# Two-layer decoder trunk: the prompt attention's fill bank is copied out in another order, its second query unit is taken out in two pieces, and some pooling products move into the last head pair

## The reference, cut to what matters

```python
pv, pg, c_q, c_kv, k_r, ag, mg_pool, mg_attn = split_in(x @ w_in)
b_pool = pool_branch(v_ext, pos, pg, pool_w, pool_scale) @ pool_up
q_nope, q_rope, lat, k_rope = mla_qk(c_q, c_kv, k_r, pos, ...)
o = mla_prompt(...)  # or mla_sample(...)
b_attn = (o * jax.nn.silu(ag)) @ attn_up
sub = (sigmoid(mg_pool) * b_pool + sigmoid(mg_attn) * b_attn) @ w_out
return layer_norm(DN_ALPHA * x + sub + sigmoid(x @ ple_gate) * (p_i @ ple_proj), ln_g, ln_b)
```

## Time and profile before

| what | value |
|---|---|
| three executions | 2037.77, 2044.54, 2045.38 us (median 2044.54) |
| the profiled execution | 2032.2 us, its span 2030.4 us |
| instructions | 31146 |
| PE busy | 1912.3 us (94%) |
| DVE, POOL, ACT busy | 905.2, 737.0, 565.4 us |
| mean granted clock of TensorE | 0.98 |

### The profile page before, as it was taken

The page is one execution under the profiler, slowest core; times in us unless marked ns, Lnnn a source line. Parts: engine busy times, 40 slices in busy tenths (PEclk is TensorE's granted clock), DMA queues, the critical chain, the costliest instruction groups (busy, mean ns, idle before and its releaser), DMA issues.

```text
span 2030.4 us, 31146 instructions
## 1 busy us (share of the span) xinstructions
PE 1912.3 (94%) x12391; PEld 1816.3 (89%) x12391; DVE 905.2 (45%) x1484; ACT 565.4 (28%) x997; POOL 737.0 (36%) x743
## 2 busy tenths in 40 slices
PE   6999899999999999999989989999999999999994
PEld 5998888888799999999989968888878999999994
DVE  4344566664164111535454535666623721134216
ACT  6123444443122010201251334444421310120002
POOL 3332343342145333434244322343312443334434
PEclk9999999999999999999999999999999899999997
DMA  5213221053812221222132141121365122222222
GB/s 212 74 47 131 65 64 62 22 177 123 288 34 62 78 66 56 89 89 68 30 128 55 41 165 33 55 64 61 138 234 181 32 89 72 67 68 87 66 67 84
DMA packets 94746, 183.96 MB, mean 91 GB/s; under 512 B 12086, under 2 KB 35942, under 8 KB 93964
## 3 DMA queue, kind: packets, MB, share of 16 engines
q1 hardware_dynamic: 73440, 135.43, 21.7%
q10 hardware_dynamic: 21180, 46.80, 6.1%
HBM read 150.19 MB, written 32.45 MB: 90 GB/s over the span
## 4 chain that ended last, share of the span: by engine, by line
PE 73%; DVE 11%; ACT 9%; issue 3%; ACTq 1%; DMA 1%; POOL 1%; DVEq 0%; SPq 0%; POOLq 0%
PE PS L615 52%; PE PS L710 5%; PE PS L638 4%; PE PS L595 4%; DVE MX L1662 3%; ACT PB L1243 2%; ACT PTH L1047 2%; DVE PTL L1650 2%; PE PS L695 2%; PE PS L730 1%; PE PS L671 1%; DVE PS L1661 1%; PE PS L754 1%; DMA RAW<-in_wstream 1%; ACT FST L1047 1%
## 5 line engine op out<-in xcount | busy, mean ns | idle before, releaser
L512 POOL CAST WH<-RAW 128x512 fp32r<-128x512 f32 (+3 forms) x292 | 200.7, 687 | 905.8 <-DMA RAW<-in_wstream 905.8
L514 POOL TENSOR_TENSOR WL<-RAW,WH 128x512 fp32r<-128x512 f32 (+3 forms) x292 | 382.2, 1309 | 23.5
L615 PE MATMUL PS<-XH,WH 128*128 128x344 f32 x1344 | 290.0, 324 | 4.6 <-ACT SGB L1283 3.9
L615 PE MATMUL PS<-XL,WH 128*128 128x344 f32 x1344 | 287.4, 322 | 0.0
L615 PE MATMUL PS<-XH,WL 128*128 128x344 f32 x1344 | 286.8, 322 | 0.0
L615 PEld LDWEIGHTS PS<-XH,WH 128*128 128x128 f32 x1344 | 228.0, 190 | 7.3 <-ACT SGB L1283 4.5
L615 PEld LDWEIGHTS PS<-XH,WL 128*128 128x128 f32 x1344 | 227.5, 189 | 0.0
L615 PEld LDWEIGHTS PS<-XL,WH 128*128 128x128 f32 x1344 | 227.3, 190 | 0.0
L533 POOL TENSOR_SCALAR PB<-PB,RC 128x128 f32<-128x128 f32 (+7 forms) x128 | 96.1, 751 | 333.3 <-DVE RC L1644 333.3
L638 PE MATMUL PS<-XH,WH 128*128 128x344 f32 x384 | 127.4, 332 | 29.1 <-ACT FST L1047 29.1
L1243 ACT ACTIVATE PB<-PS,NB 128x128 f32<-128x128 f32 (+7 forms) x128 | 95.0, 742 | 188.2 <-DVE NB L1663 187.9
(11 more groups left out here) (275 smaller groups left out, 3860.2 us busy)
## 6 DMA issues: line engine op xcount, KB each, us to landing
RAW<-in_wstream SPq DMA_DIRECT2D x236, 256.0 KB, 2.7
PAGES<-in_pages SPq DMA_DIRECT2D x128, 320.0 KB, 4.9
spill_p<-PST ACTq DMA_DIRECT2D x16, 516.0 KB, 2.9
spill_g<-FST ACTq DMA_DIRECT2D x48, 172.0 KB, 1.9
SGL<-spill_g ACTq DMA_DIRECT2D x16, 516.0 KB, 4.4
PRJ<-spill_p ACTq DMA_DIRECT2D x16, 516.0 KB, 4.4
spill_v<-VSTG ACTq DMA_DIRECT2D x16, 512.0 KB, 2.8
VSP<-spill_v SPq DMA_DIRECT2D x8, 1024.0 KB, 5.3
```

The costliest lines, as they stand in the source:

```text
L512: pool.tensor_copy(WH[:, slot, 0:size], RAW[:, slot, 0:size]).then_inc(w_high[slot], 1)
L514: pool.tensor_tensor(WL[:, slot, 0:size], RAW[:, slot, 0:size], f(WH[:, slot, 0:size]), ALU.subtract).then_inc(w_split[slot], 1)
L615: last = nc.tensor.matmul(PS[:, 3 * par + c, 0:CH], w[:, slot, at], x(k)[:, c * CH:(c + 1) * CH], start=(k == 0 and n == 0), stop=(k == kt ...
```

## The change

The second query unit's third bank (344 columns) is multiplied first and counts `q_rot` alone; then the banks 0 and 1 (688 columns) in a second instruction. PE waits for the first of them, runs the first 8 fill matmuls, fill(-2), ahead of scores(1), and the other 16 behind it. The fill bank's chunks are copied on ACT in the steps 2, 4, 7, 10, 13, 16 and not 2, 5, 8, 11, 14, 16; chunk 0 ahead of PTH(0) and not behind it. The spill DMA is issued behind exp(n). In the last pair of a layer 14 of the 24 pooling products stand ahead of values(7).

```diff
-        PV_FIRST = 24
+        PV_HEAD, PV_FIRST = 14, 24
-        FILL_AT = {-1: (0, 24)} | {n: (24 + 8 * n, 32 + 8 * n) for n in range(15)}
-        FILL_EVAC = {2: 0, 5: 1, 8: 2, 11: 3, 14: 4, 16: 5}
+        FILL_AT = {-2: (0, 8), -1: (8, 24)} | {n: (24 + 8 * n, 32 + 8 * n) for n in range(15)}
+        FILL_EVAC = {2: 0, 4: 1, 7: 2, 10: 3, 13: 4, 16: 5}
...
                     scores(l, i, 0)
+                    pe.wait_ge(q_rot, 3 * r + 2)
+                    fill(l, i, -2)
                     scores(l, i, 1)
                     fill(l, i, -1)
...
                     if i < PAIRS - 1:
                         keys_unit(i + 1)
+                    else:
+                        pv_fill(l, (0, PV_HEAD))
                     values(r, GROUPS - 1)
...
-                pv_fill(l, (0, PV_FIRST))
+                pv_fill(l, (PV_HEAD, PV_FIRST))
...
                     copy(FST[:, b, :], PS[:, FILL_BANK, 0:CH]).then_inc(fill_free, 1)
+
+                def fill_spill(l, i, chunk):
+
+                    r, b, c = l * PAIRS + i, chunk % 2, chunk % 3
                     act.wait_ge(fill_free, 6 * r + chunk + 1)
-                    c = chunk % 3
                     act.dma_start(SPILL_G[...], FST[:, b, :]).then_inc(fill_out[b], 16)
...
-                        act.wait_ge(q_rot, 2 * r + h + 1)
+                        act.wait_ge(q_rot, 3 * r + 2 * h + 1)
...
                     for n in range(18):
                         m = n - 2
+                        if n == 2:
+                            fill_evac(l, i, 0)
...
-                        if n in FILL_EVAC:
+                        if n in FILL_EVAC and n > 2:
                             fill_evac(l, i, FILL_EVAC[n])
                         if n < 16:
...
+                        if n in FILL_EVAC:
+                            fill_spill(l, i, FILL_EVAC[n])
...
-                        own(v.tensor_tensor(thirds(QRAW[:]), bank_set(1 - h), thirds(TAB[:]), ALU.mult))
+                        if h == 0:
+                            own(v.tensor_tensor(thirds(QRAW[:]), bank_set(1), thirds(TAB[:]), ALU.mult))
+                        else:
+                            v.tensor_tensor(QRAW[:, 2 * CH:T], PS[:, FILL_BANK, 0:CH], TAB[:, 2 * CH:T], ALU.mult
+                                            ).then_inc(q_rot, 1)
+                            own(v.tensor_tensor(thirds(QRAW[:])[:, 0:2, :], bank_set(0)[:, 0:2, :], thirds(TAB[:])[:, 0:2, :],
+                                                ALU.mult))
+                            dve.wait_ge(q_rot, 3 * r + 2)
```

## The result

The changed kernel takes **2015.3 us** (median of 4, 2008.9 to 2019.7) beside 2041.2 for the kernel before: ratio 0.9875, 95% interval 0.9845 to 0.9904. Two later comparisons gave 0.9877 (0.9843 to 0.9912; 2015.8 beside 2037.8) and 0.9881 (0.9857 to 0.9905; 2012.0 beside 2037.3). It is 22 to 26 us faster. The kernel before had come out lower too: 2041.2 here and 2035.9 to 2037.8 later, where I had started from 2044.5.

A forecast was written before the change was run, and what follows sets the result against it. It took a ScalarE, VectorE and GpSimd loop beside TensorE (94% busy) to limit what shorter TensorE waits gain. 10.0 us from the pairs plus 4.0 from the last pairs, 14.0 off 2044.5, gave 2030.5 us, range 2018 to 2042.

The forecast's parts named there:

- Parts 1 and 2: Split query product with fill(-2) between, and earlier fill-bank copies: 1.51 us a pair, 10.0 us over eight pairs.
- the loop: Chain over ScalarE, VectorE and GpSimd beside TensorE in each pair; a gain counts by how much earlier exp(n) starts.
- the hold: Step 10 of a pair: the copy on ScalarE pushes a ready exp(10) back by 0.55 us.
- The first pair: First pair of a layer: activation table load delays exp(1), first shift +0.49 not -0.46, gain only 0.45 us.
- Part 3: Spill DMA issue moved behind exp: costs nothing; without that cover 40 by 0.34, 13.6 us.
- Part 4: Last pair of each layer, 14 pooling products ahead of values(7): 2.0 us a layer, 4.0 us for both.
- Rival B: Last pair's low clock does not come, PE no longer standing still: 4.6 us more, 2026; chance 0.12.
- C: All PE waits go and the loop has slack: about 50 us faster, 1995; chance 0.03.
- D: Splitting the query product costs VectorE 0.4 more; every pair behaves like the first: 8 us, 2036.5; chance 0.22.
- E: ScalarE's wait for fill ahead of exp: 0.55 at step 10, at worst 12.4 us slower, 2057; chance 0.07.
- F: The parts do nothing, since the loop, not PE, holds each end already: 2044.5; chance 0.06.
- the new waits: Sign: PE's new waits on PTL and on the normalisation should stand at 8 to 16 us together.

The follow-up runs named there:

- Parts 2 and 3 alone: Kernel before with only the earlier fill-bank copies and the spill DMA issued behind exp: 2023.7 us beside 2037.8, ratio 0.9921.
- the mixed ones: Changed kernel with ten pooling products dealt among the 8-column matmuls, 2027.1 us; with the fill matmuls also dealt unevenly, 2022.8 us.
- Part 2 alone: Kernel before with only the earlier fill-bank copies, the spill's issue right behind its copy: 2032.5 us beside 2035.9, ratio 0.9989.
- Part 1 alone: Kernel before with only the second query unit's product in two pieces and eight fill matmuls ahead of scores(1): 2035.8 us beside 2035.9, ratio 1.0002.

## Why the prediction was wrong in size and right in sign

**Parts 1 and 2, a pair.** The method held: the loop, not PE's waits, gave each shift, and the holds sat where I had put them. Shifts against before, from the pair's start:

| landmark | predicted | measured |
|---|---|---|
| exp(2) | -0.46 | -0.56 |
| exp(3) | -0.46 | -0.81 |
| exp(6), behind step 5 | -0.71 | -1.04 |
| PTH(7) | -1.66 | -2.08 |
| exp(11), behind the hold | -1.12 | -1.58 |
| exp(12) and the pair | -1.51 | -2.02, 2.06 |

The forecast failed at two steps: a hold in the loop that this part left out, and the clock inside the pairs, which the sum did not have at all (below).

The step of the loop that failed is the sentence "Nothing in exp(2) to exp(5) is held by PE". In the kernel before PTH(1) started at 365.62, 0.81 behind exp(2) at 364.81:

```profile
364.81 0.58 ACT L1243 ACTIVATE PB<-PS,NB 128x384 f32<-128x384 f32 x1 [1.02 <-DVE NB L1663]
...
365.21 0.38 PE L671 MATMUL PS<-IDENT,PB 128*128 128x128 f32 x2
...
365.62 0.39 ACT L1047 ACTIVATE PTH<-PS 128x256 fp32r<-128x256 f32 x1
```

After the change the distance is 0.58 (360.60, 361.18). So 0.23 of it was a wait for turn(1), which PE ended at 365.59. The profile names no releaser for it, since ACT was busy with the accumulator's read up to 365.48 and only 0.14 idle: I had looked at waits with a name and not at distances between instructions. The rest of the miss is small terms: exp(2) 0.10, step 8 1.03 for 0.95, the hold 0.50 for 0.55, step 12 0.44 for 0.39. At step 4 I had given a spare of 0.3; the copy at 365.95 does push exp(4) there, by 0.1. All this together is 0.55 in a pair: the loop gave 14.6 us where I had 10.0.

**The first pair** won 1.11 in layer 0, not 0.45. Its exp(2) was 0.35 late from the pair's start, and not 0.49, and then the same unseen gains came. My own terms did not give 0.45 either: 1.51 less the 0.95 between -0.46 and +0.49 is 0.56. It is 70.27 where Parts 2 and 3 alone have 70.12: behind the table load the split product brings nothing.

**Part 3.** That an issue beside an exp costs nothing was right (at step 2 it starts 0.01 behind exp and lasts 0.34). The price without that cover, 40 by 0.34, was wrong both ways: it falls due only at steps 2 and 10, where the next activation is ready, and there it is 0.52, since the overlap with the copy goes too. 16 by 0.52 is 8.3.

**Part 4** was right: 2.0 a layer, 1.97 and 1.99 measured at equal low stretches. Values(7) follows the pooling products without a gap, 0.27 later where I had 0.2. The low clock came all the same, but later, over the narrow matmuls of sample 0 (1.94 for 16, where they took 1.07 before), and in layer 0 for a shorter time; that is the 1.5 more in that layer. The length varies from trace to trace: 3.4 to 13.7 us, 6.8 in the mean, over the 12 ends of a layer in the six traces without Part 4, and none to 10.2, 4.7 in the mean, over the 18 in the nine traces with it (the mixed ones left out); in one of these 18 the low clock did not come. Rival B, by which it would not come, is refuted in its form, and the stretches do get shorter. Its price rested on a misreading too: of layer 1's products at the low clock I counted 15 in 4.4 us, where the trace has 11 steps of 0.287 in 3.3.

**The term that was missing** is the clock inside the pairs. I had one such pair in the trace (72.93) and took no notice of it. The sum put it at nothing: it priced the wait of step 8 by the loop alone. The kernel before loses 1.4 to 1.6 in each pair where the clock falls behind that wait: one pair in its first trace, three in its second. The change removes the wait and with it all of them.

**The new sum**: six pairs by 2.06 and two by 1.11 are 14.6, Part 4 is 4.0: 18.6. Low stretches of the pairs, one to three, are 1.4 to 4.4, and one fewer at the end of a layer 1.5: 21.5 to 24.5, beside 22 to 26 measured. How many such stretches an average run of the kernel before has is not known beyond two traces. An estimate from the mean granted clocks of the timed runs, 0.976 before and 0.979 after: one stretch of 3.4 at half the clock takes 0.0008 off the mean of a run, so the kernel before has three to four more of them, some 5 us, and the sum comes to some 24.

**The other rivals.** C (all waits count) is refuted by Part 2 alone. D (the split costs 0.4 more) too: the pieces took 0.52 and 0.86, as worked out from the earlier trace rows. E had its place and price right, 0.50 at step 10, and never reached its deciding point. F fell. Of the signs, the new waits were to be 8 to 16 and are 19, or 23 with those that bear no name; PE got further ahead than I thought. My base of 2044.5, a median of three, was high as well: 17 to 35 runs of the kernel before gave 2035.9 to 2037.8. From 2037.5 my 14 would have given 2023.5, inside my range, so of the 15 us between 2030.5 and 2015.3 some 7 are the base and some 8 the two steps above. The chances were added wrongly as well: by their own terms "faster" is 0.60 and "within" 0.33, not 0.58 and 0.35.

The Trainium skill (TensorE: Matmul & The Clock Gate, What's actually happening) says that the default clock is the low one, that activity releases it, and that the activity is judged in windows which run free of the kernel. The traces agree: the grid of instants above runs on while the pairs shift against it, and the same 1.98 us wait brings the low clock in 24 pairs of 48, all of them where it began 0.34 to 1.56 us behind an instant, and not in the others. Run to run it is luck how many of a kernel's waits stand so.

## What to carry to other kernels

Price a wait by what it does to the loop beside it, and look for holds in the distance between two instructions of one engine, not only in the waits that bear a name. A part that is worth nothing alone (the spill's issue) can be worth 1.0 a pair once another part makes its queue the late one, so test parts in the pairs in which they touch. And count a stall of TensorE of 2 us twice: once for itself, and once for the clock behind it, which here fell in half of the cases. Read the granted clock of every period of a loop before you take one as typical.

## What was not expected of the hardware

- A wait of 1.98 us on TensorE was followed by a stretch at the 1.2 GHz level in 24 of 48 cases; in 88 pairs without a wait of more than 1.1 us there was none. One such stretch costs 1.3 to 1.6 us.
- Which of the 48 it was went by the wait's place on a regular grid of instants, which did not shift with the kernel's loop: begun 0.34 to 1.56 us behind one, the clock fell at the next (24 of 24); begun 1.68 us or more behind, it did not (0 of 24). So the length of a loop's period has a say in how often its stall is paid for twice: 7 pairs of 8 with Part 1 alone, 1 and 3 of 8 in the kernel before.
- The low clock also comes while TensorE counts as busy throughout, during or behind 32 matmuls of 8 columns in the last pair of a layer (17 of 18 ends with Part 4); ten wide ones mixed among them stretched it from 3.4 or 6.8 to 13.7 and 17.1 us.
- On ScalarE's queue a DMA issue behind a copy that it must wait for holds up the next activation, where that one is ready, by 0.52 us, not by its own 0.34. Behind an activation on which it does not depend it costs nothing.
